# The gated linear attention of a two-block transformer, made head by head in pieces between the units of its own input linear

## What is computed

```python
q, k, v, r, a_low = _split(h @ w_in, GLA_SIZES)          # 512, 512, 1024, 1024, 16 columns
log_a = log_sigmoid(a_low @ w_a2 + b_a) / 16
b = cumsum(log_a within a chunk of 64 tokens)
q_t, k_t = q * 128**-0.5 * exp(b), k * exp(-b)
inner = where(causal, q_t @ k_t.T, 0) @ v                # inside a chunk
kv = (k * exp(b_last - b)).T @ v                         # one 128x256 matrix per chunk and head
s = s * exp(b_last) + kv                                 # the state, chunk after chunk
o = inner + q_t @ s_prev
o = _head_norm(o) * silu(r)                              # mean and variance over the 256 of a head
return o @ w_out
```

## Time and profile before

| | us |
|---|---|
| kernel, median of 3 runs | 3408.16 (3408.14 to 3410.47) |
| profiled execution | 3410.03, its span 3408.2 |
| TensorE busy in the span | 3313.7 (97%) |
| mean granted TensorE clock, as a share of full speed | 0.986 |

### The profile page before, as it was taken

The page is one execution under the profiler, slowest core; times in us unless marked ns, Lnnn a source line. Parts: engine busy times, 40 slices in busy tenths (PEclk is TensorE's granted clock), DMA queues, the critical chain, the costliest instruction groups (busy, mean ns, idle before and its releaser), DMA issues.

```text
span 3408.2 us, 44206 instructions
## 1 busy us (share of the span) xinstructions
PE 3313.7 (97%) x16096; PEld 2741.6 (80%) x16096; DVE 1194.6 (35%) x1882; ACT 1171.9 (34%) x1848; POOL 1652.4 (48%) x894
## 2 busy tenths in 40 slices
PE   8999999999999999899999999999999999799998
PEld 6788888787788887888888788888888888588887
DVE  4534124445441144511344332124311433421133
ACT  4743222438442233422233432222322333232222
POOL 6735444567264445644447344444544453154443
PEclk9999999999999999999999999999999999899998
DMA  4112222221122222232222122222222222122221
GB/s 149 44 49 95 95 96 99 68 101 45 35 96 93 98 98 75 96 105 96 95 93 93 56 68 93 92 99 99 95 97 93 99 93 81 38 87 93 98 99 56
DMA packets 80800, 293.87 MB, mean 86 GB/s; under 512 B 8971, under 2 KB 9355, under 8 KB 80428
## 3 DMA queue, kind: packets, MB, share of 16 engines
q1 hardware_dynamic: 79344, 286.06, 25.0%
q10 hardware_dynamic: 1340, 6.23, 0.5%
HBM read 290.15 MB, written 2.10 MB: 86 GB/s over the span
## 4 chain that ended last, share of the span: by engine, by line
PE 88%; DVE 4%; POOL 4%; issue 3%; ACT 2%; DMA 0%; POOLq 0%; DVEq 0%; SPq 0%; ACTq 0%
PE bank L1953 27%; PE bank L1955 27%; PE bank L1954 27%; POOL diag L671 1%; PE bank L2375 1%; POOL scr L602 1%; POOL w_lo L556 1%; PE bank L2336 1%; PE bank L1999 1%; DVE mvl L1316 1%; PE bank L2356 1%; PE bank L1981 0%; PE bank L2198 0%; ACT w_hi L760 0%; PE bank L2176 0%
## 5 line engine op out<-in xcount | busy, mean ns | idle before, releaser
L556 POOL TENSOR_TENSOR w_lo<-w_raw,w_hi 128x1024 fp32r<-128x1024 f32 x537 | 1313.4, 2449 | 1534.4 <-ACT w_hi L760 1534.3
L1953 PE MATMUL bank<-mvh,w_hi 128*128 128x512 f32 (+1 forms) x4520 | 1745.0, 386 | 46.9 <-DVE mvl L1316 20.0
L1955 PE MATMUL bank<-mvh,w_lo 128*128 128x512 f32 (+1 forms) x4520 | 1721.1, 381 | 0.0
L1954 PE MATMUL bank<-mvl,w_hi 128*128 128x512 f32 (+1 forms) x4520 | 1720.5, 381 | 0.0
L760 ACT ACTIVATE w_hi<-w_raw 128x1024 fp32r<-128x1024 f32 x537 | 568.3, 1059 | 1774.2 <-PE bank L1955 1771.2
L1953 PEld LDWEIGHTS bank<-mvh,w_hi 128*128 128x128 f32 x4520 | 858.3, 190 | 231.8 <-issue 32.4
L1955 PEld LDWEIGHTS bank<-mvh,w_lo 128*128 128x128 f32 x4520 | 857.7, 190 | 161.6
L1954 PEld LDWEIGHTS bank<-mvl,w_hi 128*128 128x128 f32 x4520 | 858.9, 190 | 153.7 <-issue 0.2
L1394 DVE TENSOR_TENSOR scr<-bank,rstd_b 128x512 f32<-128x512 f32 x264 | 181.4, 691 | 994.3 <-PE bank L1955 994.1
L1411 DVE TENSOR_TENSOR mvl<-big,mvh 128x512 fp32r<-128x512 f32 x132 | 270.1, 2056 | 346.6 <-ACT mvh L890 346.6
L671 POOL TENSOR_TENSOR diag<-diag,scr 128x512 f32<-128x512 f32 (+1 forms) x137 | 156.2, 1140 | 23.3 <-ACT scr L785 13.1
(11 more groups left out here) (190 smaller groups left out, 1577.5 us busy)
## 6 DMA issues: line engine op xcount, KB each, us to landing
w_raw<-in_weights SPq DMA_DIRECT2D x537, 512.0 KB, 3.3
x<-in_x SPq DMA_DIRECT2D x8, 256.0 KB, 8.5
out_y<-y SPq DMA_DIRECT2D x4, 512.0 KB, 2.7
tab<-in_dist ACTq DMA_DIRECT2D x2, 640.0 KB
tab<-in_gmlp ACTq DMA_DIRECT2D x2, 640.0 KB
tab<-in_ret_dil ACTq DMA_DIRECT2D x1, 1280.0 KB
y<-in_p ACTq DMA_DIRECT2D x2, 512.0 KB, 3.4
y<-in_rotary ACTq DMA_DIRECT2D x1, 1024.0 KB
```

What stands on the lines that cost most here:

```text
L556: nc.gpsimd.tensor_tensor(w_lo[:, slot, :], w_raw[:, slot, :], w_hi[:, slot, :].bitcast(F32), ALU.subtract).then_inc(w_lo_ready, 1)
L1953: nc.tensor.matmul(bank[:, at], hi, mvh[:, k, at], start=first, stop=False)
L1954: nc.tensor.matmul(bank[:, at], hi, mvl[:, k, at], start=False, stop=False)
L1955: return nc.tensor.matmul(bank[:, at], lo, mvh[:, k, at], start=False, stop=last)
```

## The change

GLA's main part moves between the units of its own input linear, and goes head by head instead of block by block.

- The weight tiles are reordered on the host (`G_TILES`): unit 0 is now `a_low`, then K, Q, V, R. Nothing of their number or size changes.
- There are two places per unit: `(s, 0)` after the fourth of its 8 input tiles, and `(s, 1)` at its end. Tables of such places say what stands there; every engine does its part of a piece in the same order.
- z goes in two halves at (4, 1) and (5, 0), the exponential at (5, 1), the logarithm at (6, 0); the sums of head h at (7+h, 0), its transposed key and scores at (8+h, 1), V's tile i at (10+i, 0). Head h has `kv` at (12+2h, 1) and (13+2h, 0), its values at (13+2h, 1) and (14+2h, 0), statistics at (14+2h, 1), normalising at (15+2h, 0). The inverse root is one power on GpSimd. The transposes back and the gate stand at (18, 1), (20, 1), (22, 1) and (24, 0).
- All heads' values use banks 0 and 1; TensorE begins head h's when head h-1 is normalised (`gla_normed`).
- SiLU is made per unit of R (units 17 to 24), not four tiles at a time.
- Tiles 0 to 3 of the result's high part are written once unit 24 is past its fourth input tile (`mix_in_free`), the others after it. The output linear begins with its first four units side by side, each tile used as it comes (`gla_out`).

The core of the diff, with two lines of the tables, and then the new `gla_units` of GpSimd, `gla` of ScalarE, `gla` of VectorE, and `gla_values`, `gla_units` and the main order of TensorE:

```diff
+G_TILES = (8, 4, 5, 6, 7, 0, 1, 2, 3) + tuple(range(9, 25))
+BACK_C = (0, 1, 4, 5, 2, 3, 6, 7)
...
+        KV_AT = {(12 + 2 * h, 1): (h, 0) for h in range(GLA_H)}
+        KV_AT.update({(13 + 2 * h, 0): (h, 1) for h in range(GLA_H)})
...
+            def gla_units():
+
+                u0 = lin["b_mix_in1"].u0
+                for s in range(25):
+                    splits(u0 + RING + s + 1)
+                    if (s, 1) in STATS_AT:
+                        h = STATS_AT[(s, 1)]
+                        at = slice(4 * h, 4 * h + 4)
+                        pool.wait_ge(gla_var, h + 1)
+                        nc.gpsimd.tensor_tensor(sm_y[:, at], ret_vars[:, at], neg_half.broadcast_to([P, TB]),
+                                                ALU.pow).then_inc(gla_rstd, 1)
...
+            def gla():
+
+                for s in range(25):
+                    if s >= RING:
+                        beside_gla((s, 0))
+                    if s == 24:
+                        act.wait_ge(mix_in_free, 1)
+                        for t in range(RING):
+                            gla_high(t)
+                    gla_unit(s)
+                    if s >= RING:
+                        beside_gla((s, 1))
+                for t in range(RING, 8):
+                    gla_high(t)
...
+            def gla():
+
+                for s in range(25):
+                    if s >= RING:
+                        beside_gla((s, 0))
+                    if s == 24:
+                        gla_gate(6)
+                        gla_low(0)
+                    gla_unit(s)
+                    if s >= RING:
+                        beside_gla((s, 1))
+                gla_low(1)
+                gla_low(2)
+                gla_gate(7)
+                for t in range(3, 8):
+                    gla_low(t)
...
+            def gla_values(h, i):
+
+                if i == 0:
+                    pe.wait_ge(gsc_masked, h + 1)
+                    if h == 0:
+                        pe.wait_ge(b_used, GLA_H)
+                    ge(pe, gla_normed, h)
...
+            def gla_units():
+
+                L = lin["b_mix_in1"]
+                for s in range(RING, 25):
+                    pe.wait_ge(w_lo_ready, L.u0 + s + 1)
+                    pe.wait_ge(bank_free, L.e0 + (s - 3 if s < 6 else s - 1))
+                    for k in range(KT):
+                        last = three(banks[LIN[s % 2]], (L.u0 + s) % RING, k, k, k == 0, k == KT - 1)
+                        if k == RING - 1:
+                            if s == 24:
+                                last.then_inc(mix_in_free, 1)
+                            beside_gla((s, 0))
+                    last.then_inc(unit_done, 1)
+                    beside_gla((s, 1))
...
-                    from_x("b_mix_in1", beside_gla)
-                    pe.wait_ge(bank_free, lin["b_mix_in1"].e0 + lin["b_mix_in1"].n)
-                    pe.wait_ge(vt_copied, 28)
-                    gla()
-                    body = from_cat("b_mix_out1")[1]
-                    for i in range(KT - 1):
-                        body(0, i)
-                    last_mixed(1)
+                    from_x("b_mix_in1", units=RING)
+                    gla_units()
+                    gla_out()
```

More of the change, by code:

```diff
@@ L277, in __call__ @@
                 self.eng.wait_ge(self.s, self.n)
[L279 to L293, removed]
         def col(name, k=0, n=1):
@@ L1079, in beside_gla @@
-            def beside_gla(s):
+            def beside_gla(at):
+                for b in Z_AT.get(at, ()):
+                    act.wait_ge(z_done, b + 1)
+                    chain(nc.scalar.activation(scr[:, 4 + b, :], banks[4 + b][:, :], ACT.Abs))
                 for b in range(TB):
[L1082 to L1085, removed]
+                    if at == EXP_AT:
@@ L1100, in beside_gla @@
[L1100 to L1111, removed]
+                    nc.scalar.activation(y[:, 4 + h, :], banks[4][:, :], ACT.Copy).then_inc(kt_copied, 1)
@@ new lines, in beside_gla @@
+                if at in GV_AT:
+                    transposed_value("b1", GV_AT[at])
+                if at in NORM_AT:
+                    h = NORM_AT[at]
+                    act.wait_ge(gla_shift, h + 1)
+                    for b in range(TB):
+                        i = slice(4 * h + b, 4 * h + b + 1)
+                        c0 = b % 2 * GLA_DV
+                        last = nc.scalar.activation(gla_normal(h)[:, b * GLA_DV:(b + 1) * GLA_DV],
+                                                    banks[b // 2][:, c0:c0 + GLA_DV], ACT.Identity,
+                                                    scale=sm_y[:, i], bias=shift[:, i])
+                    last.then_inc(gla_normed, 1)
@@ new lines, in beside_gla @@
+                if at in STATS_AT:
+                    gla_stats(STATS_AT[at])
+                if at in NORM_AT:
+                    h = NORM_AT[at]
+                    i = slice(4 * h, 4 * h + 4)
+                    dve.wait_ge(gla_rstd, h + 1)
+                    nc.vector.scalar_tensor_tensor(out=shift[:, i], in0=mean_var[:, 8 * h:8 * h + 8:2], scalar=-1.0,
+                                                   in1=sm_y[:, i], op0=ALU.mult, op1=ALU.mult).then_inc(gla_shift, 1)
+                if at in TURN_AT and TURN_AT[at] < 3:
+                    for m in range(2):
+                        gla_gate(2 * TURN_AT[at] + m)
@@ L1959, in wide @@
                 L = lin[name]
-                back = [f"b_mix_out{l}" for l in range(LAYERS)]
+                mixed = name.startswith("b_mix_out")
                 def body(t, s):
@@ L1964, in body @@
                     pe.wait_ge(w_lo_ready, t * RING + L.u0 + s + 1)
-                    bank = banks[BACK[s] if name in back else LIN[s % 4]]
-                    if name not in back:
+                    bank = mix_bank(int(name[-1]), s) if mixed else banks[LIN[s % 4]]
+                    if not mixed:
                         pe.wait_ge(bank_free, t * RING + L.e0 + s - 3)
@@ new lines, in beside_gla, with gla_kv @@
+                if at in KV_AT:
+                    gla_kv(*KV_AT[at])
+                if at in O_AT:
+                    gla_values(*O_AT[at])
+                if at in TURN_AT:
+                    gla_turn(TURN_AT[at])
+            def gla_kv(h, part_n):
+                if part_n == 0:
+                    pe.wait_ge(vt_copied, 20 + 2 * h + 2)
+                    pe.wait_ge(kt_copied, GLA_H)
+                    pe.wait_ge(gsc_masked, GLA_H)
+                ge(pe, state_ready, 7 * h + 4 * part_n)
+                for n in range(4 * part_n, min(4 * part_n + 4, 7)):
+                    b, p0, c0 = n // 2, 64 * (n % 2), n // 2 % 2 * GLA_DV
+                    last = nc.tensor.matmul(banks[4 + n % 2][:, c0:c0 + GLA_DV], y[p0:p0 + 64, 4 + h, b * P:(b + 1) * P],
+                                            big[p0:p0 + 64, GV + 2 * h:GV + 2 * h + 2, b * P:(b + 1) * P],
+                                            start=True, stop=True)
+                last.then_inc(kv_done, 1)
@@ new lines, in gla_turn @@
+            def gla_turn(h):
+                pe.wait_ge(gla_normed, h + 1)
+                if h == 0:
+                    pe.wait_ge(vt_copied, 28)
+                else:
+                    pe.wait_ge(gated_ready, GATED0 + 2 * h)
+                for m in range(2):
+                    for b in range(TB):
+                        last = nc.tensor.transpose(banks[6 + m][:, b * P:(b + 1) * P],
+                                                   gla_normal(h)[:, b * GLA_DV + m * P:b * GLA_DV + (m + 1) * P],
+                                                   ident[:, :])
+                    last.then_inc(gla_turned, 1)
```

360 lines of the change are left out of this document (164 added, 196 removed).

## The result

| | us |
|---|---|
| before, median of 5 runs | 3408.14 (3407.05 to 3410.47) |
| changed kernel, median of 5 runs | 3390.97 (3390.11 to 3392.47) |
| ratio | 0.995, 95% interval 0.9935 to 0.9964 |
| profiled execution of the changed kernel | 3391.47, its span 3389.6 |

The kernel is 17.2 us faster by the medians and 18.6 by the two spans. The forecast was 3389, range 3383 to 3397.

The account below looks back on a forecast made before the run. TensorE was taken to wait, and fall to a slower clock, on an uncovered chain through VectorE and ScalarE. Removing 26.3 us and adding 7.2 of waits gives 19.1 off 3408.2: 3389 us, range 3383 to 3397.

Parts of the forecast that it names:

- What bounded the kernel: Main part, 55.4 us: TensorE waits for an uncovered chain through VectorE and ScalarE, and its clock falls after longer gaps.
- What it removes: Idle and slow time in the main part 21.8 us, half clock in the first output unit 2.6, behind z 1.9.
- The work that had to stay: TensorE's main part: kv products 10.2 us, values and state products 19.3, transposes back 4.1; sum 33.6.
- The logarithm: Middle of unit 7: TensorE waits about 1.5 us for log_a, ready 9.6 us after the end of unit 5.
- The head norm: Values of heads 1 to 3 wait for the head before to be normalised: 1.3, 1.3 and 1.7 us.
- The end: Start of the output linear: TensorE waits 1.1 to 1.7 us for low parts, taken as 1.4.
- What I took as nothing: Taking out units, splits, SiLU per unit, weight loads, four output units side by side and switching to pieces cost 0 us.
- The sum: Whole kernel: 26.3 us removed less 7.2 of new waits gives 19.1 us, off a span of 3408.2.
- The upper bound: Whole kernel: three half-clock stretches stay and waits are half as long again (3.6 us), giving 3397 us.
- Slow stretches and longer waits: Rival, between the units: slow stretches stay and waits are longer; 3392 to 3400 us, chance 0.18 for 3394 to 3400.
- The clock kept down by small pieces: Rival, units 12 to 20: small pieces keep the clock low; 3437 us at 60% slow, chance 0.02 for slower.
- The chain only moved: Rival: normalising a head takes some 15 us, so three heads wait 16 us more; 3405 us, chance 0.03.

Follow-up runs that it names:

- e2: Changed kernel with the whole main part behind the last unit again, still head by head, with the power on GpSimd and the output linear's early start; 3421.12 us.
- e6: Changed kernel with the exponential of the decay in the middle of unit 5 and VectorE's last step at (6, 0); 3386.42 us.
- e5: Changed kernel with a head's statistics at the middle of unit 14+2h, shift and normalising at its end, the power ahead of GpSimd's split; 3385.95 us.
- e7: Changed kernel with the low parts of tiles 1 and 2 made ahead of taking unit 24 out of its bank; 3385.55 us.
- e10: Changed kernel with the inverse root in 11 small steps on VectorE in place of the power on GpSimd; 3397.7 us.
- e9: The kernel with early statistics, early exponential and early low parts, but the inverse root in 11 small steps on VectorE; 3384.95 us.
- e8_three: Changed kernel with early statistics, early exponential and early low parts of tiles 1 and 2 together; 3383.23 us.

## Why the prediction was right, by its steps

**What bounded the kernel.** Right, and shown: with the same instructions back behind the units (e2) the loss returns and more, though e2 also has the new order, so 30.8 us is not the price of the missing cover alone.

**What it removes, 26.3 us.** It went: no half clock from unit 4 on, no idle time but the three kinds of wait. The work that had to stay was put at 33.6 us; transposes back cost 0.9 and not the 1.03 us per head of the earlier trace rows (a unit with them stands 6.33 us from the one before, 5.44 + 0.9), so 0.5 us too much was kept.

**The logarithm, 1.5.** 1.4 in the view of waits, 1.7 by the edit that removes it (e6). The drain behind a table load that the Trainium skill gives (ScalarE: Activation LUTs, What ACT_TABLE_LOAD costs) is not seen: ScalarE's first exponential starts at 2808.90, 1.30 after the load at 2807.60.

**The head norm, 1.3, 1.3 and 1.7.** 1.0, 1.1 and 1.4 by the distances between units (11.79 against 10.76; 11.37 and 11.63 against 10.26), 3.5 in all, 3.2 by e5. The chain was 9.3 us and not 9.7 where head 1's values wait (VectorE began the states 1.3 us after the unit's end, at 2877.16, not at 1.8), and 9.9, not 10.7, where head 3's values wait, with the two gates in it (2915.98 to 2925.84).

**The end, 1.4.** 1.76 by e7. As worked out, the low part of tile 2 ran into GpSimd's split: the two lows took 3.49 us where five take 3.08.

```profile
2961.68 3.49 DVE L1814 TENSOR_TENSOR mvl<-big,mvh 128x512 fp32r<-128x512 f32 x2
2965.10 0.68 DVE L1808 TENSOR_TENSOR big<-bank,big 128x512 f32<-128x512 f32 x1
2965.70 3.08 DVE L1814 TENSOR_TENSOR mvl<-big,mvh 128x512 fp32r<-128x512 f32 x5
```

**What I took as nothing.** Switches between unit work and pieces cost nothing for V's transposes, sums, scores, kv and values (each distance is 5.44 plus the pieces to 0.1 us), but z's pieces on 33 partitions cost 0.3 us each: 9.70 us from unit 4 to unit 5, where 5.44 and 3.62 make 9.06. The other covers at nothing held: no wait for a bank, a split or a weight.

**The sum.** Over the distance it was to be 19.1 and is 19.6: waits smaller by 0.5 in all (6.7 for 7.2), transposes by 0.5, z larger by 0.6, and a wait of 0.6 for keys between the old units, which I had not counted, gone too. These make 1.0, of which 0.5 is seen. That they nearly cancel is luck.

On the whole kernel it is 18.6 by the spans, since the last 26 us, the same instructions in both, took 0.9 longer in this execution (0.7 of it one gap ahead of GpSimd's last instruction). By the medians it is 17.2, 2.4 less than over the distance. The step that was loose is the base: the sum was set on 3408.2, the median and also the span, though the profiled execution itself had taken 3410.0; on that it gives 3390.9 (measured 3391.5 there). What the other executions lost outside the distance no trace shows, so this part of the 2 us by which 3389 was low stays open.

**The upper bound.** It was worked out too low. The 1.9 and 2.6 us are what those stretches had cost, not their lengths, so three that stay cost 1.9 + 2.6 + 2.6 = 7.1, and with 3.6 of longer waits the bound is 3400, not 3397. The result lies within either.

**The rivals.** Slow stretches and longer waits: not in this kernel, but in e10, whose waits are 2.29, 2.29 and 3.11 us, not 1.0 to 1.4. The gap of 2.22 us that I held against this rival proves little: one of e10's two waits of 2.29 was followed by half clock. The clock kept down by small pieces: out, 1.00 over 164 us, though pieces of transposes, kv and values stand in every half unit. The Trainium skill's rule on transposes (TensorE: Matmul & The Clock Gate, Part 4: PE-mode transpose) cost nothing here. In e2, without units beside them, two pieces of transposes of 1.1 us came with waits of 2.41 and 1.11 us between, and the third piece took 1.94 us; the rule and the waits would both explain that, and no run tells them apart. The chain only moved: out.

## What to carry to other kernels

A chain over several engines that TensorE waits for is laid under independent dense work by cutting both into pieces and giving each piece a place; the place of a result is then set by when the other engines' lists, in their order, can have it. Lay such a chain out in time from one unit's end, engine by engine, before measuring: each wait was found so to within 0.4 us (the head norm's one by one; its sum was 0.8 too high), and each went by moving one step ahead of work that nobody waited for. An order that is good under cover can be worse than the old one without it (e2), so the two edits belong together. Cover for the engine that waits is not room on the list of the engine that makes the chain: 2.2 us of small steps on VectorE cost about 1 us a head though no value waited for them (e9).

## What was not expected of the hardware

The instructions ahead of the change, the same in all, took different times: unit 4 was taken out between 2792.9 and 2797.0 us in the traces of these kernels. They differ in which of the earlier stretches run at half clock, as these windows of the changed kernel show, and below them the same of e5, at the end of an attention whose code is alike in both:

```profile
690.00:701.00 11.00, 10.03 (x73) 9.83 (x72) 4.30 (x10) 3.35 (x7) 6.79 (x7) 0.84 0.24 84
701.00:717.00 16.00, 11.20 (x63) 10.49 (x61) 9.88 (x18) 7.49 (x17) 8.40 (x6) 0.68 0.22 74
```

```profile
690.00:701.00 11.00, 9.10 (x73) 8.48 (x71) 5.64 (x15) 5.06 (x11) 6.26 (x7) 1.00 0.28 94
701.00:717.00 16.00, 11.33 (x74) 11.00 (x75) 9.90 (x19) 6.55 (x17) 9.85 (x9) 0.79 0.20 67
```

In the two traces of the changed kernel unit 4 is taken out at 2796.77 both times, and both have these clocks (0.84 and 0.68); so what sets it goes at least in part with the program and not only with the single execution. What it is stays open. It moves whole-kernel times by more than an edit of 1 to 2 us is worth, and was the reason to judge e5, e6 and e7 by the distance in the trace. Their medians alone claim 4.7, 4.2 and, against the changed kernel's 3390.63 measured at another time, 5.1 us, but e8_three, with all three edits, is 7.4 below it.
